# The first norm of a two-block transformer kernel on one core: no stage of constants, the next block normalised ahead, transposes copied by two engines, and projection half-tiles between the transposes

## The reference, cut to what matters

```
def first_block(x, pre_norm_w, ..., w_in, ...):
    h = rms_norm(x, pre_norm_w[l])            # x: 1024 tokens by 1024
    p = h @ w_cat                             # w_cat: w_in
    p_rwkv, p_conv, p_pool, p_gate = jnp.split(p, ...)
    p_rwkv = token_shift(p_rwkv, mu_shift[l])
    ...                                       # rwkv scan, convolution, pool, gates, w_out
    x = x + rms_norm(out, post_norm_w[l])
def reference(x, ...):
    x = first_block(x, ...)
    return second_block(x, ...)               # attention, retention, feed-forward
```

## Time and profile before

| what | value |
|---|---|
| median of 3 runs | 2578.97 us (2578.96 to 2587.96) |
| the profiled execution: its time, its span | 2582.76 us, 2580.6 us |
| mean granted clock of TensorE | 0.979 |
| busy: PE, PEld, DVE, ACT, POOL | 2461.9, 1963.8, 1085.8, 773.9, 865.5 us |
| share of PE in the span | 95% |

### The profile page before, as it was taken

How to read it: one execution, slowest core, us unless ns; L and a number is a source line. 1 busy time by engine, 2 the same in 40 slices (tenths; PEclk the granted TensorE clock), 3 DMA queues, 4 the chain that set the end, 5 groups by cost and what they waited for, 6 DMA issues and landing times. The chain is left out here.

```text
span 2580.6 us, 43595 instructions
## 1 busy us (share of the span) xinstructions
PE 2461.9 (95%) x18356; PEld 1963.8 (76%) x18356; DVE 1085.8 (42%) x1336; ACT 773.9 (30%) x1213; POOL 865.5 (34%) x517
## 2 busy tenths in 40 slices
PE   5997999999999999989999998989999999999999
PEld 4775777777777888778777886767768888887887
DVE  5444222222212434454364536744278666660000
ACT  3323222222212111143252104542354333332210
POOL 0234212222201122234363451135336545555622
PEclk8998999999999999999999999999999999999999
DMA  6245233333121111144433341022422222224431
GB/s 188 90 153 155 77 88 94 87 85 90 45 90 41 49 58 50 41 147 131 147 95 115 84 105 34 18 82 70 143 70 94 69 91 87 65 98 143 151 114 66
DMA packets 258582, 238.77 MB, mean 93 GB/s; under 512 B 35889, under 2 KB 218417, under 8 KB 258417
## 3 DMA queue, kind: packets, MB, share of 16 engines
q1 hardware_dynamic: 251536, 224.28, 27.8%
q10 hardware_dynamic: 6880, 12.06, 1.7%
HBM read 166.80 MB, written 61.90 MB: 89 GB/s over the span
## 5 line engine op out<-in xcount | busy, mean ns | idle before, releaser
L177 POOL TENSOR_TENSOR wlo<-wraw,whi 128x1024 fp32r<-128x1024 f32 x87 | 219.8, 2527 | 691.1 <-ACT whi L172 679.3
L3188 PE MATMUL tl_ps_bank<-tl_dn,tl_hid 128*128 128x512 f32 x1056 | 241.2, 391 | 2.5 <-POOL tl_dn L2888 2.5
L3188 PEld LDWEIGHTS tl_ps_bank<-tl_dn,tl_hid 128*128 128x128 f32 x1056 | 199.3, 189 | 44.3 <-issue 2.9
L1023 PE MATMUL rs_ps_bank<-hT_hi,rs_f_hi 128*128 128x512 f32 x384 | 172.2, 448 | 25.2 <-POOL rs_f_lo L787 14.9
L199 PE MATMUL br_ps_ps<-hT_hi,whi 128*128 128x512 f32 x448 | 178.4, 398 | 6.1 <-PEq L107 6.1
L172 ACT CAST whi<-wraw 128x1024 fp32r<-128x1024 f32 x87 | 91.2, 1048 | 309.7 <-PE ring L199 136.4
L199 PE MATMUL br_ps_ps<-hT_hi,wlo 128*128 128x512 f32 x448 | 176.4, 394 | 0.0
L199 PE MATMUL br_ps_ps<-hT_lo,whi 128*128 128x512 f32 x448 | 176.3, 394 | 0.0
L2726 PE MATMUL tl_ps_bank<-tl_M,tl_ophi 128*128 128x512 f32 x528 | 167.2, 391 | 0.0
L1023 PE MATMUL rs_ps_bank<-hT_lo,rs_f_hi 128*128 128x512 f32 x384 | 152.8, 398 | 0.0
L1023 PE MATMUL rs_ps_bank<-hT_hi,rs_f_lo 128*128 128x512 f32 x384 | 152.6, 397 | 0.0
(11 more groups left out here) (441 smaller groups left out, 5552.4 us busy)
## 6 DMA issues: line engine op xcount, KB each, us to landing
wraw<-in_w_in SPq DMA_DIRECT2D x78, 512.0 KB, 4.2
scratch_pg<-rs_f_out SPq DMA_DIRECT2D x48, 256.0 KB, 2.4
wraw<-in_w_out SPq DMA_DIRECT2D x24, 512.0 KB, 3.7
tl_raw<-in_w_gate SPq DMA_DIRECT2D x11, 1024.0 KB, 6.8
tl_raw<-in_w_up SPq DMA_DIRECT2D x11, 1024.0 KB, 5.3
scratch_hid<-tl_H SPq DMA_DIRECT2D x11, 1024.0 KB, 4.9
tl_hidraw<-scratch_hid SPq DMA_DIRECT2D x22, 512.0 KB, 3.3
tl_dnraw<-in_w_down SPq DMA_DIRECT2D x44, 256.0 KB, 2.7
```

The costliest lines, as they stand in the source:

```text
L177: self.nc.gpsimd.tensor_tensor(self.lo[s][:, :], self.raw[s][:, :], self.hi[s][:, :].bitcast(F32), ALU.subtract).then_inc(self.lo_ready, 1)
L1023: ins = mm(F[:, h, :], a[:, c], b[:, k, cols[h]], start=k == 0 and u == 0, stop=k == KD - 1 and u == 2)
L3188: ins = nc.tensor.matmul(bank[b][:, :], hid[k][:, x, c], dn[n % 2][:, v, :], start=k == 0 and j == 0, stop=k == FF - 1 and j == 2)
```

## The change

The stage of constants is gone; its five loads are issued in the norm stage, `ident` behind `gain`, the others behind the last `x`. The two weight tiles are loaded behind `x[2]` and `x[4]`. `xt` has four buffers and `plain` one pair of banks; ScalarE copies the first half of `plain` and VectorE the second. VectorE normalises block t + 1 ahead of its copy and low parts of block t; ScalarE measures block t + 2 behind the high parts of block t. TensorE runs the first seven slices of the first half of weight tiles n = 0 and 1 inside the norm stage: three before the normalised transposes of blocks 5 and 6, four before those of block 7, four behind them, into two banks that the next stage takes over. The next stage starts these halves at the last slice.

```diff
-def phase_constants(nc, d):
...
-def phase_norm_x(nc, d, w, hT, following):
-
+def phase_norm_x(nc, d, w, hT, early, following):
+
+    BUFFERS = 4
...
-        xt = [sh.sb(f"xt{u}", [P, KD, P]) for u in range(2)]
+        xt = [sh.sb(f"xt{u}", [P, KD, P]) for u in range(BUFFERS)]
...
-        plain = [sh.ps(f"plain{n}", [P, 4, P]) for n in range(4)]
+        plain = [sh.ps(f"plain{n}", [P, 4, P]) for n in range(2)]
...
-                        sp.dma_start(gain[:, :], d.pre_norm_w.partition_broadcast(P)).then_inc(consts, 16)
-                    if t == 2:
-                        for n in range(2):
-                            w.load(sp, n, n, following[n])
+                        sp.dma_start(gain[:, :], d.pre_norm_w.partition_broadcast(P)).then_inc(gain_in, 16)
+                        sp.dma_start(d.ident[:, :], d.const("ident")).then_inc(ident_in, 16)
+                    if t in (2, 4):
+                        w.load(sp, t // 2 - 1, t // 2 - 1, following[t // 2 - 1])
+                for to, of in ((d.sb_vecs, d.vecs), (d.blockones, d.const("blockones")), (d.ones, d.const("ones")), (d.eps, d.const("eps"))):
+                    sp.dma_start(to[:, :], of).then_inc(consts, 16)
...
                 measure(0)
+                measure(1)
                 for t in range(NB):
-                    if t + 1 < NB:
-                        measure(t + 1)
+                    if t >= BUFFERS:
+                        act.wait_ge(stored[t % BUFFERS], t // BUFFERS * 16)
+                    act.wait_ge(flipped, t * 4 + 1)
+                    nc.scalar.copy(xt[t % BUFFERS][:, 0:4, :], plain[0][:, :, :]).then_inc(xt_act, 1)
...
-                    if t in (2, 3):
-                        w.split_hi(act, t - 2, t - 2, 0)
+                    if t + 2 < NB:
+                        measure(t + 2)
+                    if t in (1, 3):
+                        w.split_hi(act, t // 2, t // 2, 0)
...
+                def normalize(t):
+                    measure(t)
                     dve.wait_ge(root, t + 1)
                     link(nc.vector.reciprocal(rstd[:, t:t + 1], rms[:, t:t + 1]))
...
+                dve.wait_ge(gain_in, 16)
+                normalize(0)
+                for t in range(NB):
+                    u = t % 2
                     if t + 1 < NB:
-                        measure(t + 1)
-                    if t >= 2:
-                        dve.wait_ge(stored[u], t // 2 * 16)
-                    for q in range(2):
-                        dve.wait_ge(flipped, t * 4 + 1 + q)
-                        nc.vector.tensor_copy(xt[u][:, 4 * q:4 * q + 4, :], plain[2 * u + q][:, :, :]).then_inc(xt_ready, 1)
+                        normalize(t + 1)
+                    if t >= BUFFERS:
+                        dve.wait_ge(stored[t % BUFFERS], t // BUFFERS * 16)
+                    dve.wait_ge(flipped, t * 4 + 2)
+                    nc.vector.tensor_copy(xt[t % BUFFERS][:, 4:8, :], plain[1][:, :, :]).then_inc(xt_dve, 1)
...
+                slices = iter([(t, k) for t in range(2) for k in range(KD - 1)])
+
+                def begin(n):
+
+                    for _ in range(n):
+                        t, k = next(slices)
+                        if k == 0:
+                            w.wait_split(pe, t)
+                        half_products(nc, w, early[t], w.slot(t), hT, k, slice(0, HALF))
+
                 pe.sem_inc(w.product, 4)
+                pe.wait_ge(ident_in, 16)
                 for t in range(NB):
                     pe.wait_ge(x_in[t], 16)
-                    if t >= 2:
-                        pe.wait_ge(lo, t * 2 - 2)
-                    for src, banks in ((x[t], plain), (xn[t % 2], normal)):
+                    if t:
+                        pe.wait_ge(xt_act, t)
+                        pe.wait_ge(xt_dve, t)
+                    for src, banks, first in ((x[t], plain, 0), (xn[t % 2], normal, 2 * (t % 2))):
                         if src is not x[t]:
+                            if t == NB // 2 + 1:
+                                pe.wait_ge(lo, NB)
+                            begin((0, 0, 0, 0, 0, 3, 3, 4)[t])
                             pe.wait_ge(normed, t + 1)
+                            if t >= 2:
+                                pe.wait_ge(lo, t * 2 - 2)
...
+                begin(4)
...
-        ps = [sh.ps(f"ps{n}", [P, HALF]) for n in range(4)]
+        ps = [early[0], sh.ps("ps1", [P, HALF]), early[1], sh.ps("ps3", [P, HALF])]
...
-                        for k in range(KD):
+                        for k in range(KD - 1 if n < 2 and h == 0 else 0, KD):
                             ins = half_products(nc, w, ps[2 * (n % 2) + h], w.slot(n % 2), hT, k, half[h])
```

More of the change, by code:

```diff
@@ L247, in phase_norm_x @@
         xn = [sh.sb(f"xn{u}", [P, D]) for u in range(2)]
-        xt = [sh.sb(f"xt{u}", [P, KD, P]) for u in range(2)]
+        xt = [sh.sb(f"xt{u}", [P, KD, P]) for u in range(BUFFERS)]
         junk, gain = sh.sb("junk", [P, D]), sh.sb("gain", [P, D])
         total, var, rms, rstd = (sh.sb(n, [P, NB]) for n in ("total", "var", "rms", "rstd"))
-        plain = [sh.ps(f"plain{n}", [P, 4, P]) for n in range(4)]
+        plain = [sh.ps(f"plain{n}", [P, 4, P]) for n in range(2)]
         normal = [sh.ps(f"normal{n}", [P, 4, P]) for n in range(4)]
-        consts = sh.sem("consts")
+        ident_in, gain_in, consts = (sh.sem(n) for n in ("ident_in", "gain_in", "consts"))
         x_in = [sh.sem(f"x_in{t}") for t in range(NB)]
@@ L256, in phase_norm_x @@
         flipped = sh.sem("flipped")
-        hi, lo, xt_ready = (sh.sem(n) for n in ("hi", "lo", "xt_ready"))
-        stored = [sh.sem(f"stored{u}") for u in range(2)]
+        hi, lo, xt_act, xt_dve = (sh.sem(n) for n in ("hi", "lo", "xt_act", "xt_dve"))
+        stored = [sh.sem(f"stored{u}") for u in range(BUFFERS)]
         at = lambda t: slice(t * P, (t + 1) * P)
@@ L266, in _ @@
                     if t == 0:
-                        sp.dma_start(gain[:, :], d.pre_norm_w.partition_broadcast(P)).then_inc(consts, 16)
-                    if t == 2:
-                        for n in range(2):
-                            w.load(sp, n, n, following[n])
-                for t in range(NB):
[L272 to L275, removed]
+                        sp.dma_start(gain[:, :], d.pre_norm_w.partition_broadcast(P)).then_inc(gain_in, 16)
[4 more added lines that the diff above has]
+                    sp.dma_start(to[:, :], of).then_inc(consts, 16)
+                for t in range(NB):
+                    sp.wait_ge(xt_act, t + 1)
+                    sp.wait_ge(xt_dve, t + 1)
+                    sp.dma_start(d.xT[:, :, at(t)].rearrange("k p s -> p k s"), xt[t % BUFFERS][:, :, :]).then_inc(stored[t % BUFFERS], 16)
+                sp.wait_ge(consts, 64)
+                for u in range(BUFFERS):
+                    sp.wait_ge(stored[u], NB // BUFFERS * 16)
             @block.gpsimd
@@ L317, in _ @@
                         dve.wait_ge(flipped, 4 * t - 4)
-                    nc.vector.scalar_tensor_tensor(xn[u][:, :], x[t][:, :], rstd[:, t:t + 1], gain[:, :],
+                    nc.vector.scalar_tensor_tensor(xn[t % 2][:, :], x[t][:, :], rstd[:, t:t + 1], gain[:, :],
                                                    ALU.mult, ALU.mult).then_inc(normed, 1)
+                dve.wait_ge(gain_in, 16)
+                normalize(0)
+                for t in range(NB):
+                    u = t % 2
                     if t + 1 < NB:
-                        measure(t + 1)
-                    if t >= 2:
-                        dve.wait_ge(stored[u], t // 2 * 16)
-                    for q in range(2):
-                        dve.wait_ge(flipped, t * 4 + 1 + q)
-                        nc.vector.tensor_copy(xt[u][:, 4 * q:4 * q + 4, :], plain[2 * u + q][:, :, :]).then_inc(xt_ready, 1)
+                        normalize(t + 1)
[3 more added lines that the diff above has]
+                    nc.vector.tensor_copy(xt[t % BUFFERS][:, 4:8, :], plain[1][:, :, :]).then_inc(xt_dve, 1)
                     for q in range(2):
@@ L344, in _, with phase_rwkv_in @@
                                 c = (4 * q + k) * P
-                                ins = nc.tensor.transpose(banks[2 * (t % 2) + q][:, k, :], src[:, c:c + P], d.ident[:, :])
+                                ins = nc.tensor.transpose(banks[first + q][:, k, :], src[:, c:c + P], d.ident[:, :])
                             ins.then_inc(flipped, 1)
+                begin(4)
 def rwkv_in_source(d, t):
     return columns(d.w_in, 16 if isinstance(t, int) and t == 12 else t)
-def phase_rwkv_in(nc, d, w, hT, R, following):
+def phase_rwkv_in(nc, d, w, hT, R, early, following):
     order = [12] + [base + c for c in range(4) for base in (4, 0, 8)]
@@ L3256, in program @@
         d.rms = whole.enter_context(nc.sbuf_tensor("rms", [P, S], F32))
-        phase_constants(nc, d)
-        with ExitStack() as first, ExitStack() as rings:
```

(9 more changed lines are left out.)

## The result

The changed kernel takes 2563.84 us (median of 5 runs, 2559.76 to 2565.44). The kernel before, beside it and with two more runs than were known at first, takes 2584.61 (2578.96 to 2588.57). The ratio is 0.9921, interval 0.9909 to 0.9932: 0.8% faster, clear of the 0.5% bound. The forecast of 2562.5 is 1.3 us off. Part of that closeness is luck. The median of three that it was set against, 2578.97, was low; set against the median of five, the same 16.5 us of gain would have given 2568.1, 4.3 too high. The profiled executions, for which the 16.5 were worked out, differ by 2582.76 - 2563.09 = 19.7: the sum was 3.2 short.

What follows compares the result with a forecast made beforehand. TensorE's queue was taken to bound most of the kernel; 5.6 us (projection starts earlier) plus 10.9 (fewer matmuls there) gave 16.5 us, from the median 2578.97 to 2562.5 us, range 2559.5 to 2565.

Steps and rivals of the forecast that it cites:

- What bounds the kernel; that the rest moves along: Whole kernel: mostly a TensorE queue, busy 95% of the span, so bringing the first dense matmuls forward moves all that follows.
- given back later: Later stages: where the clock falls depends on when bursts come, a few us either way; 2567 if 4 or 5 lost; chance 0.08.
- No stage of constants: Kernel start: first load issued at 0.74 instead of 4.98, 4.24 us earlier, so block 0's square starts at 4.2.
- Next block ahead, copies divided: Norm stage: pitch about 4.0 us at high clock, 4.5 to 4.6 at low; block 7 scaled at 36.1, 9.5 us earlier.
- Half-tiles inside: Norm stage: 42 of 96 projection matmuls run early; next stage starts 5.6 us earlier, then takes 12.6 us instead of 23.5.
- The 1.4 us for the low clock: Projection start: part of the 10.9 us saved there, from a clock that fell in a pause of 4.3 us before.
- What is late next: Projection: third weight tile's low part ready 11.2 us after stage start, wanted at 12.6; tanh at 11.5, wanted at 12.2.
- the second rival: Projection start: third weight tile takes 9.3 us to land, TensorE waits about 2.5 to 3 us, time 2565.5; chance 0.09.
- Cold between blocks: Norm stage: TensorE pauses of 2.0 to 2.5 us drop the clock; gain 13.0 or 11.6 us instead of 16.5; chance 0.20.
- Slower: Norm stage: single plain bank pair and ScalarE round trip allow no overlap, 9.0 us a block, time about 2602; chance 0.03.

Runs made afterwards that it cites:

- not ahead: Changed kernel with VectorE normalising each block at the head of its own turn, ScalarE measuring one block ahead; low-rank products at 57.16 us, ratio 0.9923.
- slices first: Changed kernel with half-tile slices moved ahead of the plain transposes: ratio 0.9910, again 0.9920; with two of block 7's four slices moved behind its transposes, 0.9914.

## Why the prediction was right, by its own steps

*What bounds the kernel; that the rest moves along.* Right: 19.0 at the landmark, 19.3 in the span. In other executions clock falls later on add or take some 3 us (3.4 more in the changed kernel's second, beyond its 0.2 at the landmark; 3.3 in the kernel with four `xt` and no stage). The rival "given back later" named such a loss; it came, but not in this pair, and nothing shows that the change causes it.

*No stage of constants.* 4.24 predicted; 3.4 when taken back from the changed kernel, 4.7 when added to the one before with four `xt`. Landing times were right to 0.2 us.

*Next block ahead, copies divided.* This holds the term that was mis-sized. The pitch was put at 4.0 at the high clock; it was 3.61 where nothing else held it (21.50 to 25.11), so the 0.3 us that the prediction added to VectorE's 3.7 for hand-offs was not there. The two turns that it charged with a split of a weight tile (4.6 and 4.65) took 3.87 each. The low clock it had right for block 1 but kept for block 2 as well, where the clock rose; that turn was 4.4 against 4.5. So block 5's plain transposes start at 27.34 instead of 29.3, and block 7 is scaled 11.8 us earlier instead of 9.5: by the kernels in between, 3.8 from four `xt`, 4.7 from the stage of constants and 3.3 from the rest, where the prediction had 3.1, 4.24 and some 2. The first matmul of the projection came at 44.32 instead of 46.7, nearly all of the 2.5 us that the sum lacked at the landmark. Of these 2.4, 2.0 are the earlier start of TensorE's list at block 5; block 7's own scaling, with 4.2 us on it in the kernel "not ahead", moved the end by 0.4. The text also credits the order with the cold blocks. The experiments give the order and the division together 0.6 us.

*Half-tiles inside.* The walk had right that the high parts of block 5 come late, that TensorE ends the stage, and that about one us of barrier follows (43.2 to 44.32). It had one more pause of about 0.5 us in TensorE's list, before the plain transposes of block 6 (33.4 to 33.9); the pause came before those of block 7 (0.54), and the list from block 5 on took 15.9 us instead of 16.3. Then 12.6 predicted and 12.45 measured for what is left. The 1.4 us for the low clock was 2.4 in the experiment without half-tiles.

*What is late next.* The low part of the third weight tile was ready at 55.1, the tanh at 55.3, both ahead of 56.77; the second rival didn't come.

*Cold between blocks.* It did not happen in two executions of the changed kernel. It did in seven of eleven of its neighbours: the kernel before with four `xt`, the same with no stage, not ahead, both copies on VectorE in either order, and two of three with slices first. So a chance of 0.20 was not too much. Its price was: 3.5 us were put on it, but a cold block lengthened a turn by 0.7 us (4.76 instead of 4.05) in the four kernels with the old order, and with slices first the fall at block 4 cost 1.6. The section "HAM oscillation" of the Trainium skill's page "TensorE: Matmul & The Clock Gate", which weighed against the change, describes bursts that each start at half rate behind waits for data; the waits of its example are longer than the pauses between these blocks. The trace agrees in part: behind pauses of 1.4 to 2.3 us the bursts of those seven were at half rate once or twice each, and the changed kernel's, behind 2.30 and 1.93, were not (eight transposes in 1.06).

*Slower.* The ring without overlap did not close: 3.6 to 4.55 us a block.

## What to carry to other kernels

Fill a stage that leaves TensorE half idle with matmuls of the next stage: here it moved 9.5 us of work, kept the clock high for what follows, and was about half of the gain. Before crediting a new order on another engine, ask which engine's list ends the stage; 4 us on VectorE were worth 0.4. Two edits may be needed only for each other: normalising ahead cost 2.4 us until the copies were divided, and only the two edits alone and together showed it.

## What the runs showed of the hardware

The granted clock fell to 1.2 GHz behind pauses of only 1.4 to 2.3 us, in some executions and not in others of the same kernel, and once with no pause, behind products two columns wide. What a fall cost depended on who set the pace: nothing that could be read where VectorE did (turns of 4.2 us before and across it), 0.7 us a block in the old order, 1.6 with slices first, and 1.4 to 2.4 in a dense run of matmuls, which start every 0.427 us then instead of 0.227.

At the head of the projection the clock was low in all four executions where TensorE had paused 4.3 to 4.6 us before it (before, both kernels built up from it, no half-tiles), and high in all eight with a pause of 0.9 to 1.1. Behind 1.8 us it stayed up once and fell once.

At the very start the record says 1.00 while eight transposes take 1.97 us, the time they take at a recorded 0.50; the window from 4.20 has 1.00 and begins with such transposes at 6.67; there the durations are to be trusted, not the record.
